# The convolutions' states on ScalarE's own DMA queue in a two-layer decoder step

## The reference

```python
hn = rmsnorm(x, norm1_g) * (1.0 + sc1) + sh1
xr, yr, ga, gb, gate_a, gate_b = split(hn @ w_in)
xc, rc_new = causal_depthwise_conv(xr, rc_state[l], rg_conv_w, rg_conv_b)    # 4 taps, 3 old inputs
hseq, h_last = rg_lru(xc, h_state[l], ...)
ya = (gelu(yr) * hseq) @ w_branch_a
u = ga * sigmoid(gb)
v, cc_new = causal_depthwise_conv(u, cc_state[l], cc_dw_w, cc_dw_b)          # 31 taps, 30 old inputs
v = silu(layernorm(v, cc_ln_g, cc_ln_b))
yb = v @ w_branch_b + b_branch_b
m = sigmoid(gate_a) * ya + sigmoid(gate_b) * yb
x = x + (1.0 + g1) * (m @ w_out)
x = x + (1.0 + g2) * (swiglu or top-2-of-8 experts)(rmsnorm(x, norm2_g) * (1.0 + sc2) + sh2)
```

## Time and profile before

| what | value |
| --- | --- |
| median of 3 runs | 1525.41 us (1521.86 to 1526.21) |
| the profiled execution, its time | 1527.1 us |
| its span in the profile | 1525.2 us |
| mean granted TensorE clock | 0.953 |
| PE busy | 1390.1 us, 91% |
| DVE busy | 703.3 us, 46% |
| ACT busy | 398.8 us, 26% |
| POOL busy | 364.9 us, 24% |
| DMA queue 1 (SP's), share of 16 engines | 66.4% |

### The profile page before, as it was taken

How to read it: one execution, slowest core, us unless ns; L and a number is a source line. 1 busy time by engine, 2 the same in 40 slices (tenths; PEclk the granted TensorE clock), 3 DMA queues, 4 the chain that set the end, 5 groups by cost and what they waited for, 6 DMA issues and landing times.

```text
span 1525.2 us, 27847 instructions
## 1 busy us (share of the span) xinstructions
PE 1390.1 (91%) x11878; PEld 1040.1 (68%) x11878; DVE 703.3 (46%) x1459; ACT 398.8 (26%) x641; POOL 364.9 (24%) x169
## 2 busy tenths in 40 slices
PE   4798998989799999995999979896899999999996
PEld 2697878757599998995997966575455544554443
DVE  3457765732444444335789694225322232212324
ACT  4232473230323333224344732102100000100001
POOL 1478776000000000004889750000100000000000
PEclk9899998999999999997999999996899999999998
DMA  9865433395287665445544229469299999999961
GB/s 392 217 265 186 184 112 114 89 92 198 92 322 270 251 234 182 137 125 102 148 125 150 87 83 90 135 204 368 65 386 370 377 383 383 382 378 370 386 247 36
DMA packets 169951, 332.32 MB, mean 218 GB/s; under 512 B 58480, under 2 KB 133616, under 8 KB 161808
## 3 DMA queue, kind: packets, MB, share of 16 engines
q1 hardware_dynamic: 168576, 327.68, 66.4%
q0 software_dynamic: 1296, 3.54, 0.7%
HBM read 326.06 MB, written 5.13 MB: 217 GB/s over the span
## 4 chain that ended last, share of the span: by engine, by line
PE 75%; DVE 8%; POOL 6%; SPq 4%; DMA 3%; ACT 3%; issue 1%; DVEq 0%; ACTq 0%; POOLq 0%
PE ps L793 17%; PE ps L609 12%; PE ps L580 10%; PE ps L582 9%; PE ps L581 9%; PE ps L817 8%; POOL wlo L508 4%; PE ps L619 2%; PE ps L781 2%; SPq L425 2%; POOL prod L528 2%; DMA raw<-in_stream 2%; PE ps L627 1%; PE ps L635 1%; SPq L401 1%
## 5 line engine op out<-in xcount | busy, mean ns | idle before, releaser
L580 PE MATMUL ps<-xn_hi,whi 128*128 128x320 f32 x1120 | 358.5, 320 | 53.8 <-DVE xn_lo L1099 34.0
L508 POOL TENSOR_TENSOR wlo<-raw,whi 128x1024 fp32r<-128x1024 f32 x96 | 240.4, 2523 | 533.6 <-ACT whi L852 533.5
L581 PE MATMUL ps<-xn_lo,whi 128*128 128x320 f32 x1120 | 352.1, 314 | 0.0
L582 PE MATMUL ps<-xn_hi,wlo 128*128 128x320 f32 x1120 | 351.9, 314 | 0.0
L580 PEld LDWEIGHTS ps<-xn_hi,whi 128*128 128x128 f32 x1120 | 215.8, 193 | 74.7 <-issue 34.2
L581 PEld LDWEIGHTS ps<-xn_lo,whi 128*128 128x128 f32 x1120 | 216.1, 193 | 0.2
L582 PEld LDWEIGHTS ps<-xn_hi,wlo 128*128 128x128 f32 x1120 | 215.7, 193 | 0.0
L852 ACT ACTIVATE whi<-raw 128x1024 fp32r<-128x1024 f32 x162 | 170.5, 1056 | 170.7 <-PE ps L582 115.9
L1151 DVE SCALAR_TENSOR_TENSOR ps<-upad,cols,ps 128x256 f32<-128x256 f32 x464 | 185.2, 480 | 0.0
L1099 DVE TENSOR_TENSOR wlo<-raw,whi 128x1024 fp32r<-128x1024 f32 x66 | 80.6, 1223 | 142.8 <-ACT whi L852 142.8
L793 PE MATMUL ps<-gbuf,xg 128*32 128x352 f32 x1728 | 134.9, 465 | 1.8 <-ACT row L1070 1.8
(11 more groups left out here) (227 smaller groups left out, 1432.3 us busy)
## 6 DMA issues: line engine op xcount, KB each, us to landing
raw<-in_stream SPq DMA_DIRECT2D x210, 512.0 KB, 3.7
gbuf<-in_moe SPq DMA_DIRECT2D x36, 1408.0 KB, 13.4
dbuf<-in_moe SPq DMA_DIRECT2D x36, 1408.0 KB, 14.5
ubuf<-in_moe SPq DMA_DIRECT2D x36, 1408.0 KB, 15.1
ada<-in_ada SPq DMA_DIRECT2D x24, 2048.0 KB, 8.8
out_cc<-upad SPq DMA_DIRECT2D x18, 120.0 KB, 13.3
wrg<-in_wrg SPq DMA_DIRECT2D x2, 1024.0 KB, 21.1
upad<-in_cc SPq DMA_DIRECT2D x16, 120.0 KB, 3.4
```

The lines of the kernel that those rows point to most:

```text
L508: e.tensor_tensor(wlo[:, s, :], raw[:, s, :], whi[:, s, :].bitcast(F32), ALU.subtract).then_inc(lo_pool, 1)
L580: e.matmul(out, w[0], x2[0], start=start, stop=False)
L581: e.matmul(out, w[0], x2[1], start=False, stop=False)
L582: return e.matmul(out, w[1], x2[0], start=False, stop=stop)
```

## The change

The two functions `states` and `store_states` are moved from SP's program into ScalarE's, unchanged. They are called there at these places: `states(0)` ahead of layer 0's `modulate`, `states(1)` in layer 1 behind the standard deviation and ahead of `high(b)`, `high(b + 1)` and `modulate(2)`, and `store_states(l)` behind ScalarE's sixth copy of branch A and ahead of the layer norm's mean. SP loses the calls, and its chunks follow each other without them.

```diff
             load(RING, RING + 2)
-            states(0)
             load(RING + 2, RING + 4)
...
             load(8 + 4 * (NSLICE - NA - 2), BB)
-            store_states(0)
             load(BB, WO + 4)
...
             c1 = C_LAYER[1]
-            load(DN, c1 + 4)
-            e.wait_ge(chunk_done, c1)
-            states(1)
-            load(c1 + 4, c1 + BB)
-            store_states(1)
-            load(c1 + BB, NCHUNK)
+            load(DN, NCHUNK)
...
@@ ScalarE @@
+            def states(l):
+
+                for i in range(NT):
+                    for buf, h, src in ((xrp, PR, rc_d), (upad, PC, cc_d)):
+                        e.dma_start(buf[:, i, h + TP:].rearrange("p (b t) -> p b t", b=NB)[:, :, 0:h],
+                                    src[l, :, i]).then_inc(rc_in, 16)
+
+            def store_states(l):
+                e.wait_ge(st_ready, 2 * l + 1)
+                e.dma_start(rc_o[l], rclast[:]).then_inc(out_done, 16)
+                e.wait_ge(st_ready, 2 * l + 2)
+                e.dma_start(h_o[l], hlast[:]).then_inc(out_done, 16)
+                e.wait_ge(u_made, NT * (l + 1))
+                e.dma_start(cc_o[l, :, :, 0, :], upad[:, :, TP:TP + PC]).then_inc(out_done, 16)
+                for i in range(NT):
+                    e.dma_start(cc_o[l, :, i, 1:NSEQ, :], upad[:, i, PC + TP:].rearrange(
+                        "p (b t) -> p b t", b=NB)[:, :, TS:TS + PC]).then_inc(out_done, 16)
...
                 if l == 0:
+                    e.wait_ge(ada_rows, NA)
+                    states(0)
                     modulate(0)
                 else:
                     norm_std(2, NT - 1)
+                    e.wait_ge(chunk_done, b)
+                    states(1)
                     high(b)
                     high(b + 1)
                     modulate(2)
...
                 for j in range(6):
                     evac(b + BA + j, xc[:, j, :], ACT.Copy)
                     high(b + BA + j + RING)
+                store_states(l)
                 e.wait_ge(stat_done, 4 * l + 2)
                 e.activation(mean[:], ps[4][:, 0:T], ACT.Copy, scale=1.0 / D).then_inc(ln_mean, 1)
```

More of the change, by code:

```diff
@@ L395, in _ @@
             e.dma_start(wrg[:], wrg_d[0]).then_inc(wrg_in, 16)
[L397 to L402, removed]
             e.wait_ge(ada_rows, NA)
```

## The result

The changed kernel takes 1568.59 us (median of 4 runs, 1567.83 to 1571.7) against 1525.81 us of the kernel before, measured beside it: 42.8 us or 2.87% slower (ratio 1.0287, 95% interval 1.027 to 1.0305). Forecast were 1560 us, with a range of 1538 to 1575. The span of the profiled execution is 1565.9 us, 40.7 more than before, with a granted clock of 0.945 (before 0.953).

The account below looks back on a forecast made before the run. TensorE was taken to bound the kernel (75% of the last-ending chain; moved lines 3%). Terms 24.6 + 3.2 + 6.7 = +34.5 us on the median 1525.4 gave 1560 us; own range 1552 to 1568, wider range 1538 to 1575.

Parts of the forecast that it names:

- the sum's three terms: Stores in both layers 24.6 us, loads of layer 0 3.2, loads of layer 1 6.7: together +34.5 us.
- the eight held issues: Sign: ScalarE shows eight store issues with some 18 us between branch A's sixth copy and the layer norm's mean.
- the two pauses of TensorE: Signs: pause ahead of branch B ended by `v`, not weights; new pause of 12 us or more before the squares' statistics.
- `modulate` of layer 0 near 48 us: Sign at layer 0's start: with the loads ahead of it on ScalarE, `modulate` starts near 48 us instead of 36.07.
- The stores' hold: Layer norm, both layers: store issues on ScalarE delay the mean, only 3.9 us covered; +12.3 us per layer, 24.6 in all.
- S: Time the eleven issues hold ScalarE ahead of the mean: taken as 20.0 us, bounds 7.2 and 24.
- What SP's relief gives: Ahead of branch B: without the stores SP's weights land early, first chunk ends at most 4.5 us sooner in each layer.
- The formula S - 7.7: Change per layer at branch B's first chunk, which ends at 958.1 + S against 965.85 us before.
- The loads of layer 0: Sixteen issues ahead of `modulate` take 11.8 us; split 5.5 later, 2.33 us slice wait given back: +3.2, ends +1.9 and +6.4.
- Rival (3): Longer hold: weight chunks go between the stores, ScalarE's loads pay 15.0 us; +48.9 us, about 1574 us; chance 0.09.
- The loads of layer 1: Issues behind the deviation, two pairs of line 508 on VectorE's split: +6.7 us; near nothing if missed, +9.9 with longer issues.
- Rival (1): Hold doesn't follow to ScalarE, eleven store issues cost 7.2 us: about 1526 us; chance 0.07, values between 0.10.
- Rival (2): Stores are out before the mean is wanted, in the 3.9 us gap after the sixth copy: -11.3, about 1514 us; chance 0.04.

Follow-up runs that it names:

- stores_only: Kernel before with only the stores moved to ScalarE's queue, at the changed kernel's place, loads left on SP: 1557.78 us against 1534.49 (ratio 1.016).
- long_runs: Changed kernel with each of a layer's eight stores as one 960-byte run per partition instead of eight of 120 (wrong values stored): 1537.46 us against 1534.49 (1.0023).
- stores_late: Kernel before with the stores on ScalarE behind the `Silu`, loads on SP: 1526.27 us against 1534.49 (0.9959); repeated as `stores_late_2`: 1519.95 against 1525.75 (0.9968).
- slice_behind: Changed kernel, but in layer 0 SP sends the 2 MB slice and chunks 4 to 7 only after the sixteen loads land: 1564.49 us against 1534.4 (1.0204).
- chunks_behind: Changed kernel, but only chunks 4 to 7 wait for the sixteen loads, the 2 MB slice stays ahead: 1571.55 us (ratio to the kernel before 1.0245).
- pairs_apart: Kernel before with stores on ScalarE behind the `Silu` and layer 1's loads on ScalarE behind the first two `high`: 1538.79 us against 1534.4 (1.0034).
- all_late: Kernel before with stores behind the `Silu` and loads behind `modulate` (layer 0) or `high(b + 3)` (layer 1), all on ScalarE: 1527.04 us against 1525.75 (1.0011).

## Why the prediction was right, and where a term was off

The direction, the path and two of the sum's three terms were right, and the time lies in the stated range of 1538 to 1575, but 0.6 us above the forecast's own range of 1552 to 1568. Of the signs named in it, the eight held issues (18.6 us), the mean 20.1 us behind the sixth copy, the two pauses of TensorE and the 6.7 us of layer 1's split came; `modulate` of layer 0 near 48 us did not, it starts at 56.40.

- The stores' hold. S, the time that the eleven issues hold ScalarE, was taken as 20.0 us with ends of 7.2 and 24; it is 20.8 and 20.1 (24.7 in layer 0 of `stores_only`, beyond the upper end). The terms of 12.3 us in each layer measure 13.1 and 10.7, together 23.8 against 24.6. From the mean to the `Silu` there are 14.7 and 15.4 us (15.3 taken). The first chunk of branch B took 6.3 us in layer 0 as taken, but 4.7 in layer 1. That the hold comes with the short runs is shown by `long_runs`, that the place in ScalarE's order makes it a loss by `stores_late`.
- What SP's relief gives. Taken as 4.5 us in each layer at most. In `stores_late_2` the first merge comes 3.5 and 4.2 us nearer to the sixth copy than in the trace before, and the kernel gains 5 to 6; in `stores_late` 5.0 us of late weights are given back in the two layers and 6 to 8 are left, on an occasion where the stores held SP longer.
- The formula S - 7.7 is too dear for a small S: at 6.1 it gives -1.6 us, `long_runs` had -5.1 and -4.0 (from the sixth copy to the first merge, against the trace before). It charged a slow clock where TensorE hardly stops: from the mean to the `Silu` there are 12.9 us in both layers instead of 15.3, and the granted clock is 1.00 from the statistics of the squares to the `Silu`. The first chunk took 4.7 us in layer 0 and 6.4 in layer 1.
- The loads of layer 0. This is the term of the sum that was mis-sized: +3.2 us, with ends of +1.9 and +6.4, against some +10. The step that failed is the issue time, 11.8 us from layer 1's row with an upper end of 15.0; it measures 21.3. I read the 4.40 us issue of the earlier trace rows as SP's own full queue, which ScalarE's empty one would be rid of. It is the opposite: the hold comes from what is in flight on the DMA engines, whichever queue sent it, and ScalarE issues earlier, at 35.03, when more of the slice is still ahead: the slice, sent at 30.47, took 12.0 us to land, and the load issued at 36.15 was held until 43.33. `slice_behind` and `chunks_behind` show it. Rival (3) had this direction, but with 15.0 us for its price. The rest of that step held: the undisturbed split has the pace of 0.76 us, and the wait of 2.33 us is gone.
- The loads of layer 1. +6.7 us taken for the split's end, measured 27.3 against 20.6 us behind the deviation: +6.7, issues 11.7 us (11.8 taken), both pairs of GpSimd on the split as counted.
- The other 40.7 - 41.4 = -0.7 us are small shifts that weren't forecast: +2.2 at the end, in the routing and its first expert, -2.2 and -0.7 between the places. Their cause wasn't tried; the stretch to the end is 559.4 to 562.2 us in all profiles but `pairs_apart`, so +2.2 is within what it varies by.
- Rival (1), the hold stays behind, is excluded. Rival (2) named the right mechanism for a gain: `stores_late` is that gain, got by the place and not by cheap issues. Rival (3), a longer hold by chunks of weights between the stores, did not come in the changed kernel: SP sent two chunks in that time, as it was taken there, and the hold was 20.1 to 20.8 us. The longer hold in `stores_only` is no proof of it, since on that occasion SP's own hold was longer too.

The rule that was weighed there, the Trainium skill (DMA: Bandwidth & Descriptors, Issuing engines are not separate DMA queues), has two halves. It says that an issue's time is usually small beside the transfer. Here it is 0.6 us beside 5.6 to the landing with runs of 960 bytes, and 2.3 to 2.4 us on average, up to 5.04, beside 12.3 with runs of 120: a fifth, which eight issues in a row make 19 us of the issuer's time, more than one transfer takes to land. It also says that DMAs of different engines run on the same 16 DMA engines and interleave. The trace agrees for the loads of layer 0, whose issues SP's transfers held (21.3 us against 12.5 without them), and I hadn't used it for them.

## What to carry to other kernels

In this kernel a DMA's issue cost the issuing engine what the transfers in flight, its own or another queue's, let it cost. So ask of a moved issue not which queue it is on but what stands behind it in that engine's program and what big transfer is under way when it is issued. ScalarE's own queue paid where ScalarE had a gap longer than the hold (some 40 us behind the `Silu`, 5 to 8 us gained, 8.6 with the slice put first), and cost the hold but for the 4 us that were covered where a chain waited on it. Where stores are cut into short runs, try longer runs before moving them; here that would need another layout of the state, which no run tried with the right numbers stored.

## What wasn't expected of the hardware

- ScalarE's first load was issued at 35.03 us, before its last `high` started (35.16): the issue didn't wait until the computing instructions ahead of it were done, and only later computing waited for the issues. The same shows in `stores_late` (328.06, with seven `Silu` to come) and in `all_late` (34.35, `modulate` at 37.29). So a place in the program fixes what is held, and not when the issues begin.
- A transfer in SP's queue holds issues in ScalarE's: the third and fourth load took 7.18 and 3.21 us with a transfer of 2 MB under way and four of 512 KB sent from 36.07 to 43.75, 0.70 and 0.67 in `slice_behind`, without these.
- The eight stores of 120 KB in runs of 120 bytes held their issuer from 18.4 to 28.1 us in the executions profiled, the longest beside branch B's weights; in runs of 960 bytes 4.5 to 4.8.
